# Feed-forward weights asked for during the gather of experts' rows, or behind its last row

## The chip, the core and the metric

One core of a Trainium2 chip runs the whole program in one launch. The metric is the device time in microseconds (us), the median of several executions. Engines: PE is TensorE's matmul, PEld its weight load, DVE is VectorE, ACT is ScalarE, POOL is GpSimd, SP is SyncE. SP's and POOL's queues issue DMA transfers; all of them run on the same 16 DMA engines.

## What is computed

A two-layer transformer block is followed by another two-layer block, on 256 tokens of width 1024, in float32. The part that matters here is the expert layer at the end of the first block and the feed-forward layer at the start of the second:

```python
def peer_ffn(h, w_q, sub_keys, down, up):          # per block of tokens
    q = (xb @ w_q).reshape(n, PEER_HEADS, 2, PEER_DHALF)
    ...                                            # top 16 of 128*128 experts, for each of 8 heads
    u = jnp.take(down, idx, axis=0)
    act = jax.nn.gelu(jnp.einsum('thkd,td->thk', u, xb))
    v = jnp.take(up, idx, axis=0)
    return jnp.einsum('thk,thkd->td', (gate * act).astype(v.dtype), v)
...
    return rms_norm(x, final_g)                    # end of the first block
...
x = x + 0.5 * swiglu(rms_norm_2(x, ffn_norm[0, 0]), w_gate, w_up, w_down)   # start of the second
```

Every token needs 8 x 16 rows of `down` and of `up`, in each of the two layers.

## The kernel before, in words

**The experts (`experts`, lines 1129 to 2030).** The tables `down` and `up` lie side by side in DRAM as `peer_rows`, 2048 float32 for each expert. The work is a list of 515 slots. A slot is one head, one of the two tiles of 128 tokens and one of the 16 picks: POOL issues one indirect DMA (L1337) that gathers 128 rows of 8 KB, 1 MB, into one of eight places of the ring `rows` (`ROW_SLOTS`). DVE takes the dot product of the `down` half with the normed tokens (L1894), ACT makes gelu, times the gate, times the identity (L1642, L1646, L1651), and PE multiplies the resulting diagonal with the `up` half into PSUM (L1484). When PE has done so, POOL may fetch the next row into that place. Layer 0's slots come first, then layer 1's (from `NEXT`); the last 32 slots of each head carry, in between, the query products, key scores and top-16 search (`route`) of the next head. `finish` (L1838, L1840) adds the sums of a tile to `x`.

**The weight ring (`Weights`, lines 190 to 219).** All large weights pass through a ring of six blocks of 1 MB (`SLOTS`). `W.issue(sp, n)` lets SP issue the blocks up to number n - 1, in order; before block b it waits until PE has counted block b - 5 as multiplied. Layer 1's eight query blocks (`b1` to `b1 + 7`) go through the ring, and behind them the feed-forward blocks: `b_next` = `b1 + 8` is the first gate block g0, then u0, g1, u1, d0, g2, u2, d1 and so on (gate, up, down). `W.issue(sp, b1 + PH + SLOTS)` (L1306) asks for six of them, g0 to g2, each when PE is done with one more query block.

**Splitting.** A float32 block is used as a high half (`fp32r`, copied by ACT, 1.9 us) and a low half (block minus high, by DVE, 2.3 us). Those of g0 and u0 are made within the loop over the slots: high at slots `total - 17` and `total - 9` (L1755), low at `total - 15` and `total - 7` (L2020), into the buffers `halves_a` and `halves_b`, which are free when all queries are done.

**The seam.** `experts` ends its own `nc.Block()`, and all engines meet there before `second_block_start` begins the next one. In it SP first loads the row `final_g`, the head gains and the position bias (1.5 MB) and then goes on with the ring (`layers[0].issue`). PE transposes x and starts on g0. ACT writes the high half of the transposed x (L2111), DVE the low one (L2117); then ACT and DVE take the final norm of x (L2965, behind a wait for all three loads), split g1 (L2168, L2173), and DVE makes the factor that PE spreads over the partitions behind u0 (L2321, L2266). A block of PE's work there takes some 5.6 us, and PE is busy without a break until the next seam.

Of the kernel before, what the change touches and what calls it, by code (L numbers as in the profile page):

```python
# [16 lines left out]
F32 = mybir.dt.float32  # L17
U32 = mybir.dt.uint32
F32R = mybir.dt.float32r
ALU = mybir.AluOpType  # L20
# [7 lines left out]
KD = D // P  # L28
# [12 lines left out]
PH = 8  # L41
# [19 lines left out]
SLOTS = 6  # L61
SPLIT_SLOTS = 3
ROW_SLOTS = 8
# [1065 lines left out]
def experts(kit, dram, rows, vec, late_bias, shared, first_root):  # L1129
# [16 lines left out]
    nc, W = kit.nc, kit.weights  # L1146
# [12 lines left out]
    total, per_head = len(slots), NT * TOPK  # L1159
    OTHER, PAST = NEXT + EARLY * TOPK, PH + EARLY  # L1160
    turns = [(0, hh, BOTH) for hh in range(PH)] + [(1, hh, (T,)) for hh, T in singles]
# [12 lines left out]
    split_block = list(range(PH)) + [PH + 4, PH + 5, PH + 6, PH + 5, PH + 4] + [PH + 4 + hh for hh in range(EARLY, PH)]  # L1174
# [5 lines left out]
    b0 = W.used  # L1180
    b_edge, b_bands, b_pool, b_late, b1 = (b0 + PH + i for i in range(5))
    b_next = b1 + PH
    NEXT_HIGH_AT, NEXT_LOW_AT = (total - 17, total - 9), (total - 15, total - 7)
    row_landed = [kit.count(f"row_landed{i}") for i in range(ROW_SLOTS)]
    (loaded, squares, normed, turned, high, low, high_made, split, queried, emptied, scored, copied, topped, shifted, exped,
     chosen, gated, dotted, gelued, scaled, weighed, summed) = (kit.count(n) for n in (
# [25 lines left out]
    with kit.sb("rows", [P, ROW_SLOTS, 2 * D]) as ring, kit.sb("keysT", [P, 2, P]) as keysT, \  # L1212
# [52 lines left out]
        @block.sync  # L1265
        def _(sp):
            keys_in.up(sp.dma_start(keysT[:], dram["peer_keysT"][0]), 16)
            W.issue(sp, b0 + SLOTS)
            for n in range(late):
                if n == ROW_SLOTS - 1:  # L1270
                    sp.wait_ge(rows.stored.sem, 16 * len(rows.LINES))
                rows.load_late(sp, n, ring)
            sp.wait_ge(cleared.sem, 3)
            rows.biased.up(sp.dma_start(late_line[0:P:32], late_bias), 16)
            for v in range(len(rows.LATE)):
                rows.store_late(sp, v, late_line[:, v])
            sp.wait_ge(normed.sem, n0 + NT)
            sp.wait_ge(rows.stored.sem, 16 * (len(rows.LINES) + len(rows.LATE)))
            sp.wait_ge(cleared.sem, 5)
            late_in.up(sp.dma_start(factors[0:64:32], row_of(1)), 16)  # L1280
            late_in.up(sp.dma_start(factors[64:P:32], row_of(4)), 16)
            late_in.up(sp.dma_start(plain[0:64:32], dram["pool_rows"]), 16)
            late_in.up(sp.dma_start(plain[64:P:32], row_of(0)), 16)
            late_in.up(sp.dma_start(row_stage[0:64:32], row_of(2)), 16)
            late_in.up(sp.dma_start(row_stage[64:P:32], row_of(3)), 16)
            edge_moved.up(sp.dma_start(dram["edge_h"], h[SHORT:P, 0]), 16)
            W.issue(sp, b_edge + 1)
            sp.wait_ge(edge_moved.sem, 16)
            edge_moved.up(sp.dma_start(edge_h, dram["edge_h"].rearrange("t (o n) -> t o n", o=1).to_broadcast([HALO, TOPK, D])), 16)
            W.issue(sp, b_late + 1)  # L1290
            sp.wait_ge(consumed.sem, 1)
            late_in.up(sp.dma_start(row_stage[0:64:32], row_of(5)), 16)
            sp.wait_ge(scored.sem, sc0 + PH)
            keys_in.up(sp.dma_start(keysT[:], dram["peer_keysT"][1]), 16)
            W.issue(sp, b1 + EARLY - 1)
            g = group_of[0, PH - 1, 0]
            sp.wait_ge(chosen.sem, ch0 + g + 1)
            sp.wait_ge(gated.sem, ga0 + g + 1)
            for name, a in (("edge_idx", idx), ("edge_gate", gate)):
                edge_moved.up(sp.dma_start(dram[name].rearrange("h t k -> t h k"),  # L1300
                                           a[SHORT:P, 0, edge_picks].rearrange("p (h k) -> p h k", h=EARLY)), 16)
            sp.wait_ge(edge_moved.sem, 64)
            for name, a in (("edge_idx", edge_idx.bitcast(U32)), ("edge_gate", edge_gate)):
                edge_moved.up(sp.dma_start(a, dram[name].rearrange("h t k -> (t k) h"), allow_slow_non_contiguous=True), 16)
            W.issue(sp, b1 + EARLY)
            W.issue(sp, b1 + PH + SLOTS)  # L1306
            sp.wait_ge(scored.sem, sc0 + len(turns))
            tables_in.up(sp.dma_start(onehot, dram["onehot"]), 16)
            tables_in.up(sp.dma_start(table[0:N_BUCKETS, :], dram["rel_bias_2"]), 16)
            sp.wait_ge(row_copied.sem, 2 * len(SPREAD) + DIL_GROUPS)  # L1310
            kit.load(sp, dram["bias_scratch"].rearrange("(g j) n -> j g n", g=DIL_GROUPS), bias_rows)
            sp.wait_ge(loaded.sem, loaded.n)

        @block.gpsimd
        def _(pool):
# [239 lines left out]
        def _(act):  # L1555
# [46 lines left out]
            def square(T, behind):  # L1602
                act.wait_ge(updated.sem, behind)
                kit.act(nc.scalar.activation(out, x[:, T], ACT.Square, accum_out=ss[:, 0, T:T + 1]))

            def root(a, b):
                squares.up(nc.scalar.activation(ss[:, 1, a:b], ss[:, 0, a:b], ACT.Sqrt, scale=1.0 / D, bias=kit.eps))

# [23 lines left out]
            for j, (L, hh, T, k, kind) in enumerate(slots):  # L1632
# [109 lines left out]
                for ahead, i in heads_at(c, EARLY + 1):  # L1742
# [5 lines left out]
                        take_scores(PAST + ahead)  # L1748
                    if i == AT["exp"] + per_head:
                        exp(PAST + 1 + ahead)  # L1750
                if j in NEXT_HIGH_AT:
                    i = NEXT_HIGH_AT.index(j)
                    W.wait(act, b_next + i)
                    act.wait_ge(W.multiplied, b_next)
                    nc.scalar.copy((w_high, x_high)[i], W.ring[:, (b_next + i) % SLOTS, :]).then_inc(high_made.sem, 1)  # L1755
                if c == 6 * per_head + 12:
                    for g, bank in enumerate((0, 1, 3)):
                        act.wait_ge(rowed.sem, 2 * len(SPREAD) + g + 1)
                        row_copied.up(nc.scalar.copy(bias_rows[:, g, :], kit.bank[bank][0:J, :]))

        @block.vector
        def _(dve):
# [83 lines left out]
            def modulate(dst, T, factor, offset):  # L1846
                kit.dve(nc.vector.scalar_tensor_tensor(out=dst, in0=x[:, T], scalar=ss[:, 2, T:T + 1],
                                                       in1=factor, op0=ALU.mult, op1=ALU.mult))
                return nc.vector.tensor_tensor(dst, dst, offset, ALU.add)

            def mix(T):

# [32 lines left out]
            for j, (L, hh, T, k, kind) in enumerate(slots):  # L1885
# [126 lines left out]
                if c == 6 * per_head + 4:  # L2012

                    dve.wait_ge(scored.sem, sc0 + len(turns))
                    consumed.up(nc.vector.memset(table[N_BUCKETS:N_BUCKETS + 1, :], NEG))
                if j in NEXT_LOW_AT:
                    i = NEXT_LOW_AT.index(j)
                    dve.wait_ge(high_made.sem, hm0 + len(split_block) + i + 1)
                    dve.wait_ge(W.multiplied, b_next)
                    nc.vector.tensor_tensor((w_low, x_low)[i], W.ring[:, (b_next + i) % SLOTS, :], (w_high, x_high)[i].bitcast(F32),  # L2020
                                            ALU.subtract).then_inc(split.sem, 1)
                if j == total - TOPK + 5:
                    dve.wait_ge(row_copied.sem, 12)
                    finish(0, total - TOPK - 1, gain1)
# [739 lines left out]
def second_block_start(kit, dram, shared, block):  # L2764
# [11 lines left out]
    with contextlib.ExitStack() as stack:  # L2776
# [162 lines left out]
        def _(dve):  # L2939
# [17 lines left out]
            dve.wait_ge(kit.count("gains_landed").sem, 16)  # L2957
            nc.vector.tensor_tensor(gain[:], kit.gains[:, 0], kit.gains[:, 6], ALU.mult).then_inc(made.sem, 1)
            dve.wait_ge(made.sem, m0 + 1)
            turns[0].make_low(dve, range(KD))  # L2960
            dve.wait_ge(rooted.sem, r0 + 1)
            kit.dve(nc.vector.reciprocal(ss[:, 2], ss[:, 1]))
            dve.wait_ge(loaded.sem, l0 + 48)
# [1172 lines left out]
```

## Time and profile before

| what | us |
|---|---|
| median of 3 runs | 2682.25 (2679.51 to 2684.45) |
| the profiled execution: its own time | 2681.42 |
| its span in the profile | 2679.5 |
| PE / DVE / ACT / POOL busy in the span | 2372.6 / 1851.5 / 1219.6 / 646.5 |

The span is measured from the first to the last recorded instruction; 1.9 us of the execution's own time lie outside it. The page cuts the span into 40 slices of 67 us and gives for each the busy share of every engine, the clock that TensorE was granted, and the busy share and rate of the DMA engines. The rows of experts fill slices 4 to 23, the second block the rest. PE's 89% is an average over stages with different limits, so the stage is read by itself.

### The profile page before, as it was taken

Reading aid. Unit: us, or ns where it says so; the run is one execution under the profiler, and the core shown is the slowest. Engines: PE = TensorE matmul, PEld = TensorE weight load, DVE = VectorE, ACT = ScalarE, POOL = GpSimd, SP = SyncE. Lnnn points to the kernel's source line nnn. Section 1 sums busy time; section 2 is a strip of 40 time slices with the busy share of each in tenths; the row PEclk is TensorE's granted clock in tenths of the full one; section 3 lists DMA queues with packets and bytes.
Section 4 is the critical chain, followed back from the end, with each engine's and each line's share of the span. In section 5 each row is a group of like instructions: output and inputs, shape, how many; then the busy total and the mean of one; then the engine's idle time right before and its main releaser. Section 6 shows DMA issues by size and latency. Waiting matters only on the chain. (4 is left out here: it accounts for less than half of the span.)

```text
span 2679.5 us, 35243 instructions
## 1 busy us (share of the span) xinstructions
PE 2372.6 (89%) x12936; PEld 1579.1 (59%) x12936; DVE 1851.5 (69%) x3447; ACT 1219.6 (46%) x2595; POOL 646.5 (24%) x547
## 2 busy tenths in 40 slices
PE   6988788888888988888778799999999998978999
PEld 4774333433334444333333268898888887856887
DVE  4777776678667776867764666676666666797665
ACT  3443434444445544444434454456445444445543
POOL 0004444454444434455444400000000000003000
PEclk8998999999999999999999999999999998988999
DMA  9799999999999999999999945542555554313553
GB/s 390 282 387 421 403 426 427 426 427 422 425 407 415 384 421 419 426 427 427 427 424 427 427 169 187 183 160 98 173 188 178 186 187 169 117 47 117 187 185 113
DMA packets 121705, 811.26 MB, mean 303 GB/s; under 512 B 15713, under 2 KB 18825, under 8 KB 26584
## 3 DMA queue, kind: packets, MB, share of 16 engines
q0 software_dynamic: 74160, 540.05, 48.2%
q1 hardware_dynamic: 47400, 269.32, 28.0%
q8 instruction: 85, 1.39, 0.2%
q14 instruction: 60, 0.49, 0.1%
HBM read 807.12 MB, written 1.15 MB: 302 GB/s over the span
## 5 line engine op out<-in xcount | busy, mean ns | idle before, releaser
L1484 PE MATMUL bank<-rows,diag 128*128 128x512 f32 (+1 forms) x2060 | 994.7, 620 | 210.0 <-ACT diag L1651 209.4
L1894 DVE CUSTOM_DVE_ANT_0 rows<-rows,h 128x1024 f32<-128x1024 f32 (+1 forms) x512 | 620.3, 1225 | 362.5 <-DMA rows<-in_peer_rows,idx 359.5
L1484 PEld LDWEIGHTS bank<-rows,diag 128*128 128x128 f32 (+1 forms) x2060 | 372.3, 194 | 735.5 <-ACT diag L1651 414.4
L1337 POOL DMA_INDIRECT rows<-in_peer_rows,idx x512 | 611.0, 1193 | 737.8 <-PE bank L1484 680.1
L1642 ACT ACTIVATE picks<-picks 128x1 f32<-128x1 f32 (+1 forms) x512 | 103.3, 202 | 634.5 <-DVE picks L1894 627.0
L2239 PE MATMUL bank<-hT_pair,halves 128*128 128x512 f32 x864 | 307.3, 399 | 0.4 <-DVE hT_pair L2117 0.4
L2240 PE MATMUL bank<-hT_pair,halves 128*128 128x256 f32 x864 | 242.3, 280 | 0.0
L1651 ACT ACTIVATE diag<-const_table,picks 128x128 f32<-128x128 f32 (+1 forms) x512 | 205.5, 401 | 48.0 <-ACT picks L1646 0.7
L2173 DVE TENSOR_TENSOR halves<-weight_ring,halves 128x2048 fp32r<-128x2048 f32 x73 | 167.0, 2289 | 72.0 <-ACT halves L2168 71.8
L2239 PEld LDWEIGHTS bank<-hT_pair,halves 128*128 128x128 f32 x864 | 162.3, 188 | 40.9 <-DVE hT_pair L2117 1.0
L1369 PE MATMUL bank<-halves_b,halves_a 128*128 128x256 f32 x864 | 165.9, 334 | 0.0
L2240 PEld LDWEIGHTS bank<-hT_pair,halves 128*128 128x128 f32 x864 | 163.1, 189 | 0.8
L1646 ACT ACTIVATE picks<-picks 128x1 f32<-128x1 f32 (+1 forms) x512 | 150.8, 295 | 18.5
L2168 ACT CAST halves<-weight_ring 128x2048 fp32r<-128x2048 f32 x73 | 139.4, 1911 | 42.2 <-PE bank L2248 27.0
L1369 PEld LDWEIGHTS bank<-halves_b,halves_a 128*128 128x128 f32 x864 | 119.1, 190 | 55.3 <-issue 55.3
L2173 DVE TENSOR_TENSOR halves_b<-weight_ring,halves_b 128x2048 fp32r<-128x2048 f32 x36 | 82.5, 2292 | 63.9 <-ACT halves_b L2168 63.9
L2239 PE MATMUL bank<-hT_pair,halves_b 128*128 128x512 f32 x336 | 119.6, 399 | 1.5 <-DVE work L2349 1.5
L3850 POOL MEMSET weight_ring<- 128x1024 f32 x1 | 1.0, 952 | 497.3 <-PE bank L3122 497.3
L2248 PE MATMUL bank<-halves_a,hidden 128*128 128x512 f32 x320 | 103.7, 395 | 0.0
L2173 DVE TENSOR_TENSOR halves_a<-weight_ring,halves_a 128x2048 fp32r<-128x2048 f32 x36 | 82.4, 2289 | 25.1 <-ACT halves_a L2168 25.1
L2168 ACT CAST halves_a<-weight_ring 128x2048 fp32r<-128x2048 f32 x36 | 68.9, 1915 | 59.7 <-PE bank L2248 57.8
L2240 PE MATMUL bank<-hT_pair,halves_b 128*128 128x256 f32 x336 | 94.2, 281 | 0.0
(601 smaller groups left out, 3784.8 us busy)
## 6 DMA issues: line engine op xcount, KB each, us to landing
weight_ring<-in_ffn_w_gate SPq DMA_DIRECT2D x44, 1024.0 KB, 4.8
weight_ring<-in_ffn_w_up SPq DMA_DIRECT2D x44, 1024.0 KB, 4.8
weight_ring<-in_ffn_w_down SPq DMA_DIRECT2D x44, 1024.0 KB, 4.8
mod_ring<-in_mod_w SPq DMA_DIRECT2D x16, 1024.0 KB, 8.7
weight_ring<-in_peer_w_q SPq DMA_DIRECT2D x16, 1024.0 KB, 11.4
half_ring<-in_mod_w SPq DMA_DIRECT2D x24, 512.0 KB, 6.8
rows<-in_mod_w SPq DMA_DIRECT2D x12, 1024.0 KB, 11.4
weight_ring<-in_attn_w_in SPq DMA_DIRECT2D x12, 1024.0 KB, 4.8
```

Source lines behind the costliest of these rows:

```text
L1337: nc.gpsimd.indirect_dma_start(ring[:, s], None, dram["peer_rows"], bass.IndirectOffsetOnAxis(ap=idx[:, T, n:n + 1], axis=0)).then_inc(row ...
L1369: mm = nc.tensor.matmul(kit.bank[hh % 2][:, half * SEQ:(half + 1) * SEQ], w[:, k, half * P:(half + 1) * P], t[:, :, k, :], start=(k == 0 a ...
L1484: mm = nc.tensor.matmul(bank[:, :], diag[0:n, j % DIAG_SLOTS], ring[0:n, j % ROW_SLOTS, D + half * 512:D + (half + 1) * 512], start=(j in ...
L1642: gelued.up(nc.scalar.activation(its_dot, its_dot, ACT.Gelu_apprx_tanh))
L1646: scaled.up(nc.scalar.activation(its_weight, its_dot, ACT.Copy, scale=its_gate))
L1651: weighed.up(nc.scalar.activation(diag[r, j % DIAG_SLOTS], eye[r], ACT.Copy, scale=its_weight))
L1894: dotted.up(nc.vector.tensor_tensor_reduce(out=ring[r, s, 0:D], in0=ring[r, s, 0:D], in1=its_h, scale=1.0, scalar=0.0, op0=ALU.mult, op1=A ...
L2168: self.kit.nc.scalar.copy(hi, w).then_inc(self.high_made.sem, 1)
L2173: self.kit.nc.vector.tensor_tensor(lo, w, hi.bitcast(F32), ALU.subtract).then_inc(self.split.sem, 1)
L2239: nc.tensor.matmul(bank[:, :], w_hi[:, k, cols], halves.pair[:, k, :], start=(k == 0), stop=False, skip_group_check=True)
L2240: mm = nc.tensor.matmul(bank[:, SEQ:2 * SEQ], w_lo[:, k, cols], halves.hi[:, k, :], start=False, stop=(k == KD - 1), skip_group_check=True)
L2248: mm = self.kit.nc.tensor.matmul(self.kit.bank[4 + 2 * T + half][:, :], hidden[:, f % 2, s, T * P:(T + 1) * P], w[:, s, half * 512:(half + ...
```

## The change

Only g0 is still fetched during the rows. SP then waits until the last row has landed and issues u0, g1, u1 and d0; g2 follows behind the three loads of the next Block. The high half of u0 is made by ACT after its last slot (`next_high(1)`), its low half by DVE in the next Block, between the first four and the last four columns of the transposed x. The diff, cut to what does something:

```diff
-    NEXT_HIGH_AT, NEXT_LOW_AT = (total - 17, total - 9), (total - 15, total - 7)
+    NEXT_HIGH_AT, NEXT_LOW_AT = total - 17, total - 15
...
             W.issue(sp, b1 + EARLY)
-            W.issue(sp, b1 + PH + SLOTS)
+            W.issue(sp, b1 + PH + 1)
             sp.wait_ge(scored.sem, sc0 + len(turns))
...
             sp.wait_ge(loaded.sem, loaded.n)
+            last = (total - 1) % ROW_SLOTS
+            sp.wait_ge(row_landed[last].sem, L0[last] + 16 * ((total - 1) // ROW_SLOTS + 1))
+            W.issue(sp, b_next + 5)
...
+            def next_high(i):
+                W.wait(act, b_next + i)
+                act.wait_ge(W.multiplied, b_next)
+                nc.scalar.copy((w_high, x_high)[i], W.ring[:, (b_next + i) % SLOTS, :]).then_inc(high_made.sem, 1)
...
-                if j in NEXT_HIGH_AT:
-                    i = NEXT_HIGH_AT.index(j)
-                    W.wait(act, b_next + i)
-                    act.wait_ge(W.multiplied, b_next)
-                    nc.scalar.copy((w_high, x_high)[i], W.ring[:, (b_next + i) % SLOTS, :]).then_inc(high_made.sem, 1)
+                if j == NEXT_HIGH_AT:
+                    next_high(0)
...
+            next_high(1)
...
+            def next_low():
+                dve.wait_ge(high_made.sem, hm0 + len(split_block) + 1)
+                dve.wait_ge(W.multiplied, b_next)
+                nc.vector.tensor_tensor(w_low, W.ring[:, b_next % SLOTS, :], w_high.bitcast(F32), ALU.subtract).then_inc(split.sem, 1)
...
-                if j in NEXT_LOW_AT:
...
+                if j == NEXT_LOW_AT:
+                    next_low()
...
-            turns[0].make_low(dve, range(KD))
+            turns[0].make_low(dve, range(4))
+            layers[0].make_low(dve, 1)
+            turns[0].make_low(dve, range(4, KD))
```

## Rows read from the trace of the kernel before

**Rows 1.** The page, 40 slices of 67 us: DMA busy tenths, then GB/s.

```profile
DMA  9799999999999999999999945542555554313553
GB/s 390 282 387 421 403 426 427 426 427 422 425 407 415 384 421 419 426 427 427 427 424 427 427 169 187 183 160 98 173 188 178 186 187 169 117 47 117 187 185 113
```

**Rows 2.** Windows of layer 1's rows: us, busy us, PEclk, DMA share, GB/s.

```profile
1075.00:1100.00 25.00, 17.70 (x49) 7.62 (x48) 24.38 (x78) 8.57 (x28) 10.71 (x8) 1.00 1.01 426
1112.88:1192.92 80.04, 66.72 (x189) 30.46 (x188) 57.50 (x137) 35.52 (x107) 39.49 (x33) 1.00 1.01 427
...
1425.00:1450.00 25.00, 21.13 (x46) 8.05 (x46) 11.94 (x19) 10.20 (x32) 13.07 (x12) 1.00 1.01 426
```

**Rows 3.** Timeline of SyncE's queue: start us, us, what it issued.

```profile
1024.23 0.43 SPq L214 DMA_DIRECT2D weight_ring<-in_ffn_w_gate  x1
1058.32 0.33 SPq L214 DMA_DIRECT2D weight_ring<-in_ffn_w_up  x1
...
1353.52 0.33 SPq L214 DMA_DIRECT2D weight_ring<-in_ffn_w_gate  x1
```

**Rows 4.** Row gathers (L1337) issued in 1100:1150 us, then in 1450:1550.

```profile
DMA to landing us min/median/max: 10.6/13.5/15.8
...
DMA to landing us min/median/max: 13.7/15.0/15.0
```

**Rows 5.** Timeline of the last rows and the seam.

```profile
1532.28 1.88 ACT L1755 CAST halves_b<-weight_ring 128x2048 fp32r<-128x2048 f32 x1
...
1536.13 2.29 DVE L2020 TENSOR_TENSOR halves_b<-weight_ring,halves_b 128x2048 fp32r<-128x2048 f32 x1
...
1547.26 1.23 DVE L1894 CUSTOM_DVE_ANT_0 rows<-rows,h 128x1024 f32<-128x1024 f32 x1 [1.25 <-DMA rows<-in_peer_rows,idx]
...
1549.70 1.23 DVE L1894 CUSTOM_DVE_ANT_0 rows<-rows,h 128x1024 f32<-128x1024 f32 x1 [1.21 <-DMA rows<-in_peer_rows,idx]
...
1552.05 1.98 PE L1484 MATMUL bank<-rows,diag 128*128 128x512 f32 x4 [0.46 <-ACT diag L1651]
...
1554.07 1.29 DVE L1838 TENSOR_TENSOR hT<-bank,vectors 128x512 f32<-128x512 f32 x2 [3.13 <-PE bank L1484]
1555.39 1.23 DVE L1840 TENSOR_TENSOR x_res<-x_res,hT 128x1024 f32<-128x1024 f32 x1
1557.13 0.36 SPq L187 DMA_DIRECT2D work<-in_final_g  x1
...
1557.17 1.06 PE L2104 MATMUL bank<-const_table,x_res 128*128 128x128 f32 x8 [3.14 <-PEq L1216]
```

**Rows 6.** Blocks issued back to back near 2446 us: first, fourth.

```profile
L214 SPq DMA_DIRECT2D weight_ring<-in_rw_wo x1: 350/350/350, 2446.3 to 2446.3; - x1
...
DMA to landing us min/median/max: 4.9/4.9/4.9
...
L214 SPq DMA_DIRECT2D weight_ring<-in_rw_wo x1: 752/752/752, 2447.6 to 2447.6; - x1
...
DMA to landing us min/median/max: 10.9/10.9/10.9
```

**Rows 7.** Windows of the next Block's start, columns as before.

```profile
1562.00:1564.00 2.00, 2.00 (x9) 1.81 (x8) 0.56 (x2) 1.43 (x4) 0.00 (x0) 0.50 1.08 382
...
1566.00:1568.00 2.00, 2.00 (x13) 1.73 (x12) 0.01 (x1) 1.97 (x5) 0.00 (x0) 1.00 0.00 1
```

**Rows 8.** Timeline of VectorE, and one row of TensorE, at the next Block.

```profile
1563.44 1.66 DVE L2117 SCALAR_TENSOR_TENSOR hT_pair<-bank,joined_gain,hT_pair 128x256 fp32r<-128x256 f32 x4 [2.72 <-ACT hT_pair L2111]
...
1568.20 2.48 DVE L2965 SCALAR_TENSOR_TENSOR x_res<-x_res,ss,work 128x1024 f32<-128x1024 f32 x2
1570.60 2.29 DVE L2173 TENSOR_TENSOR halves<-weight_ring,halves 128x2048 fp32r<-128x2048 f32 x1
...
1573.26 0.49 DVE L2321 TENSOR_SCALAR spread_factor<-const_table,factors 128x128 f32<-128x128 f32 x2
...
1574.62 0.60 PE L2266 MATMUL bank<-spread_factor,ones 128*128 128x128 f32 x4
```

More of the change, by code:

```diff
@@ L2015, in _ @@
                     consumed.up(nc.vector.memset(table[N_BUCKETS:N_BUCKETS + 1, :], NEG))
-                if j in NEXT_LOW_AT:
[L2017 to L2021, printed above, removed]
+                if j == NEXT_LOW_AT:
+                    next_low()
                 if j == total - TOPK + 5:
```

## The prediction

> **What bounds the kernel now.** I read the page's slices first: where the rows are gathered, the DMA engines are busy throughout at 422 to 427 GB/s, in the slices on either side of the last one before the seam as in the others, and the rate falls below 190 when the second block starts [rows 1]. The windows of layer 1's rows say the same at a finer grain: DMA share 1.01 and 426 or 427 GB/s, whether DVE is nearly full (24.38 of 25 us), PE works on queries, or no weight block is under way (1425 to 1450). Over one whole head, 80.0 us, PE is busy 66.7 us and DVE 57.5 [rows 2]. The gather is so paced by bytes moved. A block or a row of 1,048,576 bytes costs 1.0486 MB / 427 GB/s = 2.46 us of that pace, and the last rows are indeed taken up 1547.26, 1549.70: 2.44 us apart, each time after a wait for DMA [rows 5].
>
> SP's queue shows where the feed-forward blocks fall: g0 at 1024.23, u0 at 1058.32, then g1, u1, d0, and g2 last at 1353.52 [rows 3]. All five that move are issued inside the stretch in which the DMA engines never pause.
>
> At the seam the order of things is: last row taken up by DVE at 1549.70, its last matmuls 1552.05 to 1554.03, `finish` on DVE to 1556.62, all engines meet, first transposes 1557.17 [rows 5]. From there PE is the bound for the rest of the kernel.
>
> **Removed from the gather: five fetches.** 5 x 2.46 = 12.3 us, if the time that they leave is filled with rows. It is, if the queue of rows is never empty. The ring holds eight rows; a gather issued in the last stretch lands after 13.7 to 15.0 us, and where route and queries hold the ring back, after 10.6 at the least [rows 4]. Alone a 1 MB block lands in 4.9 us [rows 6]. So even there 10.6 - 4.9 = 5.7 us of other work stood ahead of the row, and one block less takes away 2.46 of it: 3.2 remain. PE and DVE could go as fast: a head without a weight block is 32 rows, 32 x 2.46 = 78.6 us, against 66.7 us of PE and 57.5 of DVE [rows 2]. The bounds are 0 (nothing refilled) and 12.3; nearest is the whole, since no row shows a pause. I take 12.3.
>
> Here a rule can be weighed. The Trainium skill (DMA: Bandwidth & Descriptors, Rules for kernel authors) says to issue a DMA early, compute, and wait late, so that its fixed cost is covered; this change does the reverse. What the rule would make of it is the third rival below. The same page of the skill (Specifications) puts HBM's share for one core at about 358 GB/s; the windows show 427 sustained, and by 358 five blocks would be 14.6 us instead of 12.3. The measurement decides.
>
> **Removed from the slots: one split.** ACT's cast at 1532.28 (1.88 us) and DVE's subtraction at 1536.13 (2.29 us) no longer stand between slots [rows 5]. Rows 1547.26 and 1549.70 still waited for DMA, so this cover is complete: 0. Without that cover it would be worth up to 2.3.
>
> **Added: SP's wait for the last row, four issues behind it.** Behind the wait on SP stands nothing but these and the end of the Block; SP's earlier loads of this Block are done. Times here are in the clock of the trace before; all of it shifts with the rows. SP wakes with DVE, at about 1549.7, and issues u0 at about 1549.8. The trace has four blocks issued back to back on a quiet queue: the first lands after 4.9 us, the fourth, issued 1.4 us later, after 10.9, so 12.3 after the first issue [rows 6], that is in order and 2.46 apart. u0 then lands at 1554.7, g1 at 1557.2, u1 at 1559.6, d0 at 1562.1. The four issues take about 2 us, over long before the engines meet.
>
> **Moved: u0's high half to the end of ACT's part.** It starts when u0 has landed: 1554.7 + 1.9 = 1556.6, and DVE's `finish` ends at 1556.62 [rows 5]. The meeting moves by 0.0; the bounds are 0 and 1 us (landing later than those 4.9).
>
> **Moved: u0's low half into the next Block.** 2.29 us on DVE, between L2117's two groups. DVE stood idle 2.72 us there, from 1560.72 to 1563.44, waiting for ACT [rows 8]. It fits with 0.4 to spare: 0. If it did not fit it would hold back the last four columns, and PE with them, by up to 2.3. The half itself is ready at 1563.0; PE wants it when g0's products end, about 5.6 us before the spread at 1574.62, so at 1569.
>
> **What is late next: the loads of the next Block.** SP issues `final_g` at 1557.13 and the gains and bias right behind [rows 5]. Their data was over by 1566, when the window shows 1 GB/s [rows 7]. Now it stands behind u1 and d0 in the same queue: d0's data ends about 1 us before it lands, at 1561, where before the loads could start at 1558. That is 3 us later (bounds 2 and 5): landed at 1569 to 1571 where DVE wanted all three at 1568.20 for L2965 [rows 8]. So DVE is held d = 0.5 to 2.9 us, I take 1.5. Behind it on DVE stand g1's low half and the factor, ready at 1573.75; PE's spread takes the factor up at 1574.62 [rows 8]. So 0.9 is cover and the stall on PE is d - 0.9: 0 to 2.0, value 0.6. g1's low half (end 1572.89 + d) is wanted only behind the spread, u1, d0 and g2 are wanted over 5 us later each; d0 and g2 have landed by then. 0 for these.
>
> **The clock.** PE stands for 3.14 us at the seam, and its granted clock is 0.50 (1.2 GHz) at 1562 to 1564, back at 1.00 (2.4 GHz) from 1566 [rows 5, 7]. The idle stretch ahead stays as long as it was, so I take the same course: 0. It can go otherwise: some 6 us at half clock are 3 us of work, given back if it doesn't fall.
>
> **Sum.** -12.3 (five fetches) + 0 (splits) + 0 (meeting) + 0.6 (loads of the next Block) = -11.7. The profiled span goes from 2679.5 to 2667.8 and its own time from 2681.42 to 2669.7. The median of the runs is 0.8 above the profiled execution: 2682.25 - 11.7 = 2670.5.
>
> **Rivals.**
> First, a gather that pauses. Where queries and route delay the ring, the DMA engines run dry once 2.46 us of weights are gone, and half of the gain is lost: -12.3 + 6.2 + 0.6 = -5.5, 2676.7. For it: DVE at 24.38 of 25 us in one window. Against: the 3.2 us still queued, and the stretch from 1425 on, without blocks, at full rate. 10%.
>
> Second, the four fetches share the engines instead of going in order, and u0 lands with d0, at 12.3 after the issue: 1562.1, cast to 1564.0, the meeting 7.4 us late, net -4.9: 2677.3. Against it: blocks of one queue landed 4.9 and 12.3 after the first issue. 8%.
>
> Third, the change does not do what it says, because the fetches cost the rows nothing and are only uncovered now: 0 + 0.6, 2682.9, no difference. This is what the rule of the skill quoted above amounts to. Against: a full DMA share in all windows of the gather. 5%.
>
> Fourth, the clock does not fall at the seam: 3 us more, -14.7, 2667.5. 6%.
>
> Fifth, on the other side: the loads behind the blocks. The position bias goes in runs of 1 KB, 1536 of them. If each took a turn as long as an 8 KB run of a block (8192 B x 16 / 427 GB/s = 0.31 us, 96 on each engine, 29 us), it would land at about 1591 and DVE would be held 22.8 us: -12.3 + 22.8 - 0.9 = +9.6, 2691.9. It decides from a delay of 12.3 + 5.4 + 0.9 = 18.6 us on. Against: alone they were through in 8 us, and in one queue they come after the blocks, not among them. 2%.
>
> **How the numbers follow.** The forecast has the remaining 69%, with a range of its own from 2670 (no stall) to 2673 (stall 2.0 and meeting 1 late). The whole range runs from the fourth rival to just past the first, 2666.5 to 2677: 85% of the chances lie in it, without the second, third and fifth. A measurement of this kernel tells a change from none at 0.2%, 5.4 us: faster 0.93 (forecast, first, second, fourth), same 0.05, slower 0.02.
>
> **What would show it.** Layer 1's windows stay at 426 or 427 GB/s, and the last row is taken up at 1549.7 - 12.3 = 1537.4. SP issues four blocks at 1537.5 to 1539.5, the first lands after 4.9 us. Transposes begin 12.3 us earlier, at 1544.9, and each us less is a us that the gather paused or the meeting waited. L2965 begins 0.5 to 2.9 us later against them than before, behind a wait for DMA, and PE's L2266 starts 12.3 - 0.6 = 11.7 earlier, at 1562.9. The prediction is wrong if a window of the gather shows less than 420 GB/s, if u0's cast ends over 1 us behind `finish`, or if L2965 waits for DMA by more than 3 us.

## The result, and the profile after

The changed kernel takes 2669.30 us in the median of 7 runs (2667.27 to 2674.21), against 2682.97 us (2679.51 to 2685.88) of the kernel before on the same chip, 7 runs: 13.7 us less. The ratio is 0.9950, 95% interval 0.9940 to 0.9959, or 11.0 to 16.1 us. The prediction was 11.7 us less, 2670.5, with a range from 2666.5 to 2677. Its profiled execution takes 2669.8 us, with a span of 2667.9 where 2667.8 was forecast.

The page of the changed kernel, its slices of the span, DMA busy tenths and GB/s (answers to [rows 1]):

```profile
DMA  9799999999999999999999965542555554213553
GB/s 383 283 386 415 403 427 427 426 427 422 425 412 420 374 426 406 426 427 427 427 423 427 427 232 188 188 158 95 183 183 186 185 184 177 105 50 118 185 187 112
```

The gather looks as it did; slice 24, with 232 GB/s where 169 stood, now holds the blocks that moved behind the last row. Windows of layer 1's rows, columns as in [rows 2]:

```profile
1075.00:1100.00 25.00, 17.71 (x48) 7.59 (x47) 24.38 (x78) 8.80 (x28) 10.69 (x8) 1.00 1.01 427
...
1125.00:1150.00 25.00, 17.54 (x40) 6.69 (x38) 24.33 (x77) 8.52 (x30) 11.32 (x11) 1.00 1.01 426
1425.00:1450.00 25.00, 19.22 (x40) 6.77 (x40) 12.22 (x19) 8.79 (x30) 9.32 (x10) 1.00 1.01 427
```

Still 426 or 427 GB/s, though g1, asked for at 1112.88 before, is no longer fetched there; the DMA engines found rows to fetch instead. Over the whole way from g0's issue to the last row both kernels have a mean of 422 GB/s. Even where DVE was busy 24.38 of 25 us the rate did not fall. So the gather ends when its bytes are through, and there are fewer of them.

The last rows and the seam in the changed kernel's timeline (answers to [rows 5]; L1905 is the dot product, L1487 the row's matmul, L1612 the cast of u0, L2111 the transposes):

```profile
1537.19 1.23 DVE L1905 CUSTOM_DVE_ANT_0 rows<-rows,h 128x1024 f32<-128x1024 f32 x1 [1.22 <-DMA rows<-in_peer_rows,idx]
...
1539.63 1.23 DVE L1905 CUSTOM_DVE_ANT_0 rows<-rows,h 128x1024 f32<-128x1024 f32 x1 [1.21 <-DMA rows<-in_peer_rows,idx]
1539.66 0.35 SPq L214 DMA_DIRECT2D weight_ring<-in_ffn_w_up  x1
...
1541.00 0.62 SPq L214 DMA_DIRECT2D weight_ring<-in_ffn_w_down  x1
...
1541.98 1.98 PE L1487 MATMUL bank<-rows,diag 128*128 128x512 f32 x4 [0.46 <-ACT diag L1659]
...
1544.43 1.90 ACT L1612 CAST halves_b<-weight_ring 128x2048 fp32r<-128x2048 f32 x1 [2.51 <-DMA weight_ring<-in_ffn_w_up]
1545.32 1.23 DVE L1846 TENSOR_TENSOR x_res<-x_res,hT 128x1024 f32<-128x1024 f32 x1
1547.05 0.33 SPq L187 DMA_DIRECT2D work<-in_final_g  x1
...
1547.10 1.94 PE L2111 MATMUL bank<-const_table,x_res 128*128 128x128 f32 x8 [3.14 <-PEq L1216]
```

The last row is taken up at 1539.63, 10.07 us earlier than before [rows 5], and SP issues u0 in the same moment, 0.03 us later. ACT waited for u0 and began its cast 4.77 us behind the issue; the cast ends at 1546.33, `finish` at 1546.55, and the first transposes start at 1547.10. That is 7.47 us behind the last row, as in [rows 5].

VectorE's timeline behind the seam, and the two rows of TensorE at the factor spread (answers to [rows 8]; L2180 at 1551.23 is the low half of u0):

```profile
1551.23 2.28 DVE L2180 TENSOR_TENSOR halves_b<-weight_ring,halves_b 128x2048 fp32r<-128x2048 f32 x1
1554.04 1.66 DVE L2124 SCALAR_TENSOR_TENSOR hT_pair<-bank,joined_gain,hT_pair 128x256 fp32r<-128x256 f32 x4 [0.52 <-ACT hT_pair L2118]
1558.59 0.17 DVE L2971 RECIPROCAL ss<-ss 128x2 f32<-128x2 f32 x1 [2.89 <-ACT ss L2889]
1558.79 2.48 DVE L2974 SCALAR_TENSOR_TENSOR x_res<-x_res,ss,work 128x1024 f32<-128x1024 f32 x2
1561.19 2.29 DVE L2180 TENSOR_TENSOR halves<-weight_ring,halves 128x2048 fp32r<-128x2048 f32 x1
...
1563.85 0.48 DVE L2328 TENSOR_SCALAR spread_factor<-const_table,factors 128x128 f32<-128x128 f32 x2
```

```profile
1563.97 0.28 PE L2247 MATMUL bank<-hT_pair,halves_b 128*128 128x256 f32 x1
1564.38 0.71 PE L2273 MATMUL bank<-spread_factor,ones 128*128 128x128 f32 x4
```

u0's low half stands in the idle stretch between the two groups of L2124, and 0.52 us of idleness are left. The final norm (L2974) starts 0.03 us behind the reciprocal: no wait for DMA. The factor is ready at 1564.33, TensorE's last product of u0 has ended at 1564.25, and the spread starts at 1564.38. Before, the spread began 0.12 us after the start of the product ahead of it (1574.50, 1574.62), now 0.41: TensorE waited some 0.3 us for the factor.

The kernel's other parts vary from one execution to the next, the stretches that the change leaves alone too: in this pair the rows ran 1.4 us late already at 1025, and the second half of the kernel made up 1.4 us. Over all the kernels below, the way from the factor spread to the end takes 1101.4 to 1111.5 us, with the same instructions in it. For a finer measure than the whole time I take, from the one profiled execution of each kernel, the way from a mark in the gather that all kernels share, the first of the last six query blocks issued by SP, to the last row's dot product. The mark in the timeline of the kernel before, and in that of the changed one:

```profile
762.16 180.23 SPq L214 DMA_DIRECT2D weight_ring<-in_peer_w_q  x4
```

```profile
763.65 181.39 SPq L214 DMA_DIRECT2D weight_ring<-in_peer_w_q  x4
```

Before: 1549.70 - 762.16 = 787.54 us. Changed: 1539.63 - 763.65 = 775.98, so 11.56 less. The second measure is the seam, from the last row's dot product to the factor spread: 1574.62 - 1549.70 = 24.92 before [rows 5, 8], 1564.38 - 1539.63 = 24.75 now.

### The profile page after: what moved, and what is told of

It reads as the page before. It is cut to its first block and busy times, and to the rows that moved or that the text cites. A ratio compares the mean times of both kernels' runs of the same rounds, so it can differ in the third digit from the quotient of the medians.

```text
span 2667.9 us, 35241 instructions
## 1 busy us (share of the span) xinstructions
PE 2367.8 (89%) x12935; PEld 1577.4 (59%) x12936; DVE 1850.8 (69%) x3447; ACT 1219.5 (46%) x2595; POOL 645.7 (24%) x547
## 5 line engine op out<-in xcount | busy, mean ns | idle before, releaser
L1487 PE MATMUL bank<-rows,diag 128*128 128x512 f32 (+1 forms) x2060 | 990.9, 618 | 201.9 <-ACT diag L1659 201.0
L1905 DVE CUSTOM_DVE_ANT_0 rows<-rows,h 128x1024 f32<-128x1024 f32 (+1 forms) x512 | 620.0, 1224 | 354.2 <-DMA rows<-in_peer_rows,idx 348.2
L1487 PEld LDWEIGHTS bank<-rows,diag 128*128 128x128 f32 (+1 forms) x2060 | 371.4, 194 | 724.5 <-ACT diag L1659 404.0
L2180 DVE TENSOR_TENSOR halves<-weight_ring,halves 128x2048 fp32r<-128x2048 f32 x73 | 166.9, 2288 | 72.2 <-ACT halves L2175 72.1
L2180 DVE TENSOR_TENSOR halves_b<-weight_ring,halves_b 128x2048 fp32r<-128x2048 f32 x37 | 84.8, 2291 | 63.8 <-ACT halves_b L2175 63.8
L2180 DVE TENSOR_TENSOR halves_a<-weight_ring,halves_a 128x2048 fp32r<-128x2048 f32 x36 | 82.4, 2289 | 25.0 <-ACT halves_a L2175 25.0
## 6 DMA issues: line engine op xcount, KB each, us to landing
weight_ring<-in_peer_w_q SPq DMA_DIRECT2D x16, 1024.0 KB, 10.7
```

Source lines behind the costliest of these rows:

```text
L1487: mm = nc.tensor.matmul(bank[:, :], diag[0:n, j % DIAG_SLOTS], ring[0:n, j % ROW_SLOTS, D + half * 512:D + (half + 1) * 512], start=(j in ...
L1905: dotted.up(nc.vector.tensor_tensor_reduce(out=ring[r, s, 0:D], in0=ring[r, s, 0:D], in1=its_h, scale=1.0, scalar=0.0, op0=ALU.mult, op1=A ...
L2180: self.kit.nc.vector.tensor_tensor(lo, w, hi.bitcast(F32), ALU.subtract).then_inc(self.split.sem, 1)
```

## The experiments

Each was timed beside the kernel before on the same chip, in three sets on three chips: the first has small_in_rows, extra_in_rows, small_at_seam and three_moved, the third changed_again, loads_between and six_between_again, the second the others; the changed kernel's own comparison stands above. Ratios of different sets are compared through the kernel before. The table has the megabytes of feed-forward weights that are fetched between the mark and the last row, the two measures from each kernel's one profiled execution, and the ratio from the timed runs with its 95% interval.

| kernel | MB in the gather | mark to last row, us | seam, us | ratio |
|---|---|---|---|---|
| before | 6 | 787.54 | 24.92 | 1 |
| split_only | 6 | 788.80 | 24.37 | 0.9995 (0.9985 to 1.0005) |
| extra_in_rows | 11 | 799.41 | 24.68 | 1.0046 (1.0033 to 1.0058) |
| asked_early | 5 | 784.18 | 24.47 | 0.9993 (0.9983 to 1.0003) |
| three_moved | 3 | 781.58 | 24.43 | 0.9967 (0.9954 to 0.9980) |
| small_in_rows | 1.3 | 774.33 | 24.75 | 0.9967 (0.9955 to 0.9979) |
| changed | 1 | 775.98 | 24.75 | 0.9950 (0.9940 to 0.9959) |
| changed_again | 1 | 776.30 | 24.75 | 0.9962 (0.9949 to 0.9975) |
| loads_between | 1 | 776.55 | 24.77 | 0.9957 (0.9942 to 0.9972) |
| small_at_seam | 1 | 774.80 | 24.76 | 0.9949 (0.9936 to 0.9961) |
| six_moved | 0 | 773.58 | 28.02 | 0.9954 (0.9941 to 0.9967) |
| six_between | 0 | 773.69 | 25.50 | 0.9950 (0.9937 to 0.9963) |
| six_between_again | 0 | 773.78 | 25.52 | 0.9952 (0.9939 to 0.9965) |

**1. The five fetches cut small, in the rows (small_in_rows).**

```diff
+            if b in self.small:
+                dst, src = dst[:, 0:1, 0:128], src[:, 0:1, 0:128]
             sp.dma_start(dst, src).then_inc(self.landed[b % SLOTS], 16)
...
+    W.small = range(b_next + 1, b_next + 6)
```

> The kernel before, with its five fetches u0, g1, u1, d0, g2 still asked for during the rows and split where they were, but each cut to 64 KB (128 columns of 512 bytes); the rest of each block is left out of the computation. Theory A (the gather pays for bytes, 2.46 us for each MB): 5 x 2.46 x 15/16 = 11.5 us faster than before, ratio 0.9957, rows at 427 GB/s to the end. Rival B (the gather pauses where queries and route hold the ring back, so half is lost): some 6 us faster, 0.998, and windows under 420 GB/s. Rival C (the fetches were hidden): no difference.

Measured: 0.9967, which is 8.9 us less (5.6 to 12.1), and the last row 13.2 us nearer to the mark. The 11.5 us of theory A lie in the interval, no difference (C) does not. By the ratio alone the 6 us of B could not be told from A; the windows of its gather, 425 or 426 GB/s from 1100 to 1500 us, speak against it, and so does the first measure. The two measures differ: the last row gained 13.2 us and the seam took 24.75, but the way from the spread to the end took 1111.5 us in this profiled execution, 6.6 more than before. The runs don't show why.

**2. The five fetches doubled (extra_in_rows).**

```diff
+            if b in self.twice:
+                self.first.up(sp.dma_start(dst, src), 16)
+                sp.wait_ge(self.first.sem, self.first.n)
             sp.dma_start(dst, src).then_inc(self.landed[b % SLOTS], 16)
...
+            W.twice, W.first = range(b_next + 1, b_next + 6), edge_moved
```

> The kernel before with the five fetches doubled: each of u0, g1, u1, d0, g2 is fetched once, SP waits until it has landed, and is fetched again into the same place. 5 MB more during the rows, nothing else changed. Theory A: 12.3 us slower, ratio 1.0046. Rival B: also 12.3 slower, since more bytes leave no pause. Rival C: no difference.

Measured: 1.0046, 12.3 us more (8.9 to 15.6), as worked out; the first measure has 11.9 more. The windows of its gather, columns as in [rows 2]:

```profile
1100.00:1200.00 100.00, 85.59 (x254) 40.64 (x253) 70.59 (x163) 44.96 (x131) 48.84 (x40) 0.98 1.01 427
1200.00:1300.00 100.00, 80.00 (x216) 35.72 (x214) 63.38 (x148) 38.45 (x117) 49.78 (x39) 0.97 1.01 427
1300.00:1400.00 100.00, 79.23 (x204) 34.87 (x204) 69.51 (x182) 38.02 (x116) 47.84 (x37) 0.95 1.01 424
```

They stand at the same 424 to 427 GB/s as before. A fetch during the rows had to be paid for, though no engine waited for it. This ends rival C.

**3. The five fetches cut small, at the seam (small_at_seam).** The edit of experiment 1 in the changed kernel.

> The changed kernel with u0, g1, u1, d0, g2 cut to 64 KB each where they are asked for now, behind the last row; the rest of each block is left out of the computation. It shows what the fetches cost at the seam. Theory A with nothing exposed there: as the changed kernel, 13 us faster than before in this comparison (0.995), within 1 us of it, and the way from the last row to TensorE's factor spread 24.5 us in place of the changed kernel's 24.75. Rival D (the fetches at the seam cost 1 to 3 us by holding back the meeting and the loads of the next Block): that much faster than the changed kernel, 0.9945 or less.

Measured: 0.9949, against 0.9950, and a seam of 24.76 us against 24.75. The ratio alone would leave room for rival D: its interval, 0.9936 to 0.9961, holds 0.9945. The seam does not: with four whole blocks behind the last row and g2 behind the loads it takes 24.75 us, with 64 KB of each 24.76. So rival D falls by the seam of the profiled executions. The 24.5 us that were expected did not come either; the 0.3 us of waiting for the factor are there without the blocks too, and belong to the clock (see below).

**4. Three blocks moved and not five (three_moved).**

```diff
-            W.issue(sp, b1 + PH + 1)
+            W.issue(sp, b1 + PH + 3)
```

> The changed kernel, but u0 and g1 are asked for during the rows again, so that three blocks move and not five; u0 is still split at the seam. Theory A: 3 x 2.46 = 7.4 us faster than before, ratio 0.9972, last row 7.4 earlier. Rival E (the gain comes from the split of u0 that no longer stands between the slots, or from the clock at the seam, and not from the bytes): the whole 12 to 13 us stay, 0.995.

Measured: 0.9967, 8.9 us less (5.4 to 12.3), expected 7.4. The last row is 6.0 us nearer to the mark than before, where 7.4 were expected. The interval overlaps that of the full change, so the ratio alone doesn't settle E; the first measure, 5.6 us short of the changed kernel's, does in part, and the next experiment does it directly.

**5. Only the split moved (split_only).**

```diff
-            W.issue(sp, b1 + PH + 1)
+            W.issue(sp, b1 + PH + SLOTS)
...
-            last = (total - 1) % ROW_SLOTS
-            sp.wait_ge(row_landed[last].sem, L0[last] + 16 * ((total - 1) // ROW_SLOTS + 1))
-            W.issue(sp, b_next + 5)
```

> The fetches as in the kernel before, all six during the rows and no wait of SP for the last row; only the split of u0 is at the seam, as in the changed kernel. Theory A (the gather pays for bytes): no difference to before, 1.000, last row where it was; DVE's 2.3 us fit into its idle stretch at the seam. Rival E (the split between the slots was what cost): several us of the gain are here already, 0.998 or less.

Measured: 0.9995 (0.9985 to 1.0005) in 12 runs: no difference that is clear of noise, at most 4.0 us of gain, and the last row is no nearer to the mark (788.80 against 787.54). Rival E wanted 0.998 or less and falls: neither between the slots nor at the seam did the split of u0 cost anything that these runs show.

**6. The blocks asked for six rows early (asked_early).**

```diff
-            last = (total - 1) % ROW_SLOTS
-            sp.wait_ge(row_landed[last].sem, L0[last] + 16 * ((total - 1) // ROW_SLOTS + 1))
+            last = (total - 7) % ROW_SLOTS
+            sp.wait_ge(row_landed[last].sem, L0[last] + 16 * ((total - 7) // ROW_SLOTS + 1))
```

> The changed kernel, but SP waits only for the seventh slot from the end, so u0, g1, u1 and d0 are asked for with six rows still queued. Theory A: these 4 MB go before the last row's end again, the last row lands some 9.8 us later than in the changed kernel, only g2 is still saved: 2.5 us faster than before, 0.999. Rival F (the DMA engines have spare time at the end of the gather, since their busy share falls over the last 5 us, and take the blocks in that time): most of the gain stays, 0.996.

Measured: 0.9993, 1.9 us less (-0.8 to 4.6), where theory A has 2.5 and F 10.7. SP's first and fourth issue in its timeline, and the dot products of some of the last rows:

```profile
1523.22 0.35 SPq L214 DMA_DIRECT2D weight_ring<-in_ffn_w_up  x1
...
1524.56 0.43 SPq L214 DMA_DIRECT2D weight_ring<-in_ffn_w_down  x1
```

```profile
1523.19 1.23 DVE L1905 CUSTOM_DVE_ANT_0 rows<-rows,h 128x1024 f32<-128x1024 f32 x1 [1.21 <-DMA rows<-in_peer_rows,idx]
...
1525.63 1.23 DVE L1905 CUSTOM_DVE_ANT_0 rows<-rows,h 128x1024 f32<-128x1024 f32 x1 [1.21 <-DMA rows<-in_peer_rows,idx]
...
1529.33 1.23 DVE L1905 CUSTOM_DVE_ANT_0 rows<-rows,h 128x1024 f32<-128x1024 f32 x1 [2.46 <-DMA rows<-in_peer_rows,idx]
...
1534.22 1.22 DVE L1905 CUSTOM_DVE_ANT_0 rows<-rows,h 128x1024 f32<-128x1024 f32 x1 [3.65 <-DMA rows<-in_peer_rows,idx]
...
1539.14 1.23 DVE L1905 CUSTOM_DVE_ANT_0 rows<-rows,h 128x1024 f32<-128x1024 f32 x1 [3.69 <-DMA rows<-in_peer_rows,idx]
...
1544.03 1.22 DVE L1905 CUSTOM_DVE_ANT_0 rows<-rows,h 128x1024 f32<-128x1024 f32 x1 [3.65 <-DMA rows<-in_peer_rows,idx]
...
1547.70 1.22 DVE L1905 CUSTOM_DVE_ANT_0 rows<-rows,h 128x1024 f32<-128x1024 f32 x1 [2.44 <-DMA rows<-in_peer_rows,idx]
```

Before the issue the rows came 2.44 us apart. With the blocks under way they are taken up at 1529.33, 1534.22, 1539.14 and 1544.03, 4.9 us apart: SP's queue and POOL's share the engines half and half. The steps from 1525.63 to the last row are 3.70, 4.89, 4.92, 4.89 and 3.67; less 2.44 each, that is 9.87 us of delay within one trace, for four blocks of 2.46 (9.84). This version is the changed kernel but for the moment at which it asks, and its last row is 8.2 us later by the first measure, which spans 780 us and scatters more.

This refutes F for six rows. Its premise holds, though: in the changed kernel the DMA engines are nearly idle over the last 4 us before the last row is taken up at 1539.63, columns as in [rows 2]:

```profile
1534.00:1536.00 2.00, 1.54 (x4) 0.68 (x4) 1.23 (x2) 0.49 (x2) 0.00 (x0) 1.00 0.57 242
1536.00:1538.00 2.00, 1.54 (x4) 0.49 (x3) 0.81 (x1) 0.90 (x3) 0.00 (x0) 1.00 0.15 61
1538.00:1540.00 2.00, 1.53 (x4) 0.49 (x3) 0.79 (x3) 0.90 (x3) 0.00 (x0) 1.00 0.06 25
```

What it would give to ask one or two rows early, into that time, no run shows.

**7. The sixth block too (six_moved).** g0 is also asked for behind the last row. The edit is cut to its main lines; left out is that PE's first transposes no longer stand behind the wait for g0's split:

```diff
-            W.issue(sp, b1 + PH + 1)
+            W.issue(sp, b1 + PH)
...
-            next_high(1)
+            next_high(0)
...
-            turns[0].make_high(act, range(KD))
+            turns[0].make_high(act, range(4))
+            layers[0].make_high(act, 1)
+            turns[0].make_high(act, range(4, KD))
...
-            turns[0].make_low(dve, range(4))
+            layers[0].make_low(dve, 0)
+            turns[0].make_low(dve, range(KD))
             layers[0].make_low(dve, 1)
-            turns[0].make_low(dve, range(4, KD))
```

> The changed kernel with g0 moved too: all six blocks behind the last row, g0's high half by ACT at the end of the experts, its low half first on DVE in the next Block, u0's high between the two groups of transposed columns, u0's low behind them; PE's first transposes no longer wait for g0's split. Theory A: last row another 2.46 us earlier, the seam longer by 0.6 (DVE's 2.3 us for g0's low half less the 1.7 it stood idle there) and up to 2 more where the next Block's loads now stand behind one block more: 12.6 to 14.2 faster than before, 0.9948 to 0.9953. Rival G (the first fetch is exposed in full at the seam): last row to factor spread longer by 3 us or more, no gain over the changed kernel or a loss.

Measured: 0.9954 (0.9941 to 0.9967), 12.3 us less, just short of the 12.6 to 14.2 expected. The last row came 2.3 us nearer to the mark (773.58, against 775.91 in the mean of the four kernels with 1 MB), but the seam grew by 3.3 us to 28.02. That is the size that rival G names; the timeline shows that it has another cause:

```profile
1542.71 1.94 PE L2106 MATMUL bank<-const_table,x_res 128*128 128x128 f32 x8 [3.14 <-PEq L1215]
1542.91 2.29 DVE L2175 TENSOR_TENSOR halves_a<-weight_ring,halves_a 128x2048 fp32r<-128x2048 f32 x1
1545.20 1.66 DVE L2119 SCALAR_TENSOR_TENSOR hT_pair<-bank,joined_gain,hT_pair 128x256 fp32r<-128x256 f32 x4
...
1554.19 0.17 DVE L2971 RECIPROCAL ss<-ss 128x2 f32<-128x2 f32 x1 [0.70 <-ACT ss L2889]
1557.66 2.48 DVE L2974 SCALAR_TENSOR_TENSOR x_res<-x_res,ss,work 128x1024 f32<-128x1024 f32 x2 [3.31 <-DMA bias<-bias_scratch]
```

The first fetch isn't exposed: the first transposes come 7.47 us behind the last row (1535.24), as in the changed kernel. Nor did g0's low half hold DVE up here: the reciprocal comes 11.48 us behind the transposes, in the changed kernel 11.49 (1547.10, 1558.59). All of the 3.3 us is the final norm, which started at 1557.66, behind a wait of 3.31 us for the position bias. One more block ahead of it in SP's queue makes the loads the last to arrive.

**8. u1, d0 and g2 behind the loads (six_between, and again; loads_between for the changed kernel).**

```diff
-            W.issue(sp, b_next + 5)
+            W.issue(sp, b_next + 3)
```

> As all six moved, but only g0, u0 and g1 are asked for ahead of the next Block's loads (final gain, head gains, position bias), and u1, d0, g2 behind them. If in the six-block version DVE waits for these loads, that wait is gone: 14.2 us faster than before, 0.9947. If it does not wait there, both are the same.

The same place in the six-block version with this edit, and then in the changed kernel with it:

```profile
1556.29 0.17 DVE L2971 RECIPROCAL ss<-ss 128x2 f32<-128x2 f32 x1 [0.70 <-ACT ss L2889]
1556.49 2.48 DVE L2974 SCALAR_TENSOR_TENSOR x_res<-x_res,ss,work 128x1024 f32<-128x1024 f32 x2
```

```profile
1558.07 0.17 DVE L2971 RECIPROCAL ss<-ss 128x2 f32<-128x2 f32 x1 [2.90 <-ACT ss L2889]
1558.27 2.48 DVE L2974 SCALAR_TENSOR_TENSOR x_res<-x_res,ss,work 128x1024 f32<-128x1024 f32 x2
```

The wait is gone, and the six-block seam is 25.50 us, 0.75 over the changed kernel's. Here the transposes take 1.06 us, and g0's low half does hold the first L2119 up: it starts at 1547.30, 2.41 us behind them, where L2117 started 1.89 behind [rows 5] before (1559.06). The ratio is 0.9950 (0.9937 to 0.9963), 13.4 us less where 14.2 were worked out, and 0.9952 when run again.

> The changed kernel once more, beside the two below. 12 to 13 us faster than before, 0.9950 to 0.9955; from the last row to TensorE's factor spread some 24.6 us.

> The changed kernel, but u1 and d0 are asked for behind the next Block's loads and only u0 and g1 ahead of them. The loads now land some 5 us earlier. In the changed kernel DVE started on the final norm without waiting for them, so this should change nothing: same time as the changed kernel. If the loads do hold DVE up in most executions, as the prediction took it (0.6 us of stall), it is up to 1 us faster.

> All six blocks moved, u1, d0 and g2 behind the next Block's loads, once more. By the bytes 2.46 us less in the gather than the changed kernel and by the first run 0.75 us more at the seam: 1.7 us faster than the changed kernel beside it, 0.9944 against 0.9950.

In the changed kernel the edit alone changes nothing: L2974 follows the reciprocal with it as without it, the seam is 24.77 against 24.75 us, and the ratio 0.9957 (0.9942 to 0.9972) against 0.9962 (0.9949 to 0.9975) of the changed kernel in the same set. That 0.9962, 10.2 us less, lies outside the 0.9950 to 0.9955 expected of it; its interval holds both. The six-block version, expected 1.7 us better (1.5 by the measures here: 2.23 in the gather less 0.75 at the seam), has a median of 2670.12 against 2671.67 beside it, and its interval, 0.9939 to 0.9965, overlaps that of the changed kernel. It can't be called faster. No version tried is shown to beat the changed kernel.

## Why the prediction was right, point by point

**The bound of the gather.** Right, though one reading was not: the DMA engines are not at 422 to 427 GB/s throughout. Seven of the twenty slices of the gather have less, down to 384 [rows 1]. They all end by 1072 us, and the first moved block was asked for at 1058; from there on the reading holds, and that is the part that the sum needs. Between 0 and 11 MB of weights the way from the mark to the last row grows from 773.7 to 799.4 us. From 6 to 1 MB it is 788.17 (mean of two kernels) less 775.91 (mean of four), 12.26 us, 2.45 a block, where the prediction had 2.46 and 12.3 in all. Other steps give less (11 to 6: 2.25 a block; 1 to 0: 2.23; asked early: 8.3 us for 4 blocks), and single kernels scatter by 1 to 2 us around a line; within one trace, asked_early has 2.47 a block.

**The queue of rows never empty.** Right where it mattered; 426 and 427 GB/s in the windows of layer 1, and the first rival's half gain did not come. The sign of being wrong, a window under 420 GB/s, was drawn too wide: the changed kernel has 405 from 1025 to 1050, where the kernel before has 421. But no moved block was fetched in that window before either, and split_only, with all six blocks in the rows, has 405 there too. From 1050 to 1530 the windows of 25 us of the changed kernel have 425 to 428 GB/s, except 417 from 1350 to 1375, where SP loads two small tables; the kernel before has 416 there.

**The splits, the meeting, u0's low half.** Each was put at 0 and came at 0 as far as the runs tell: split_only shows it for both splits together, the 7.47 us from the last row to the transposes for the meeting. The cast of u0 ended 0.22 us ahead of `finish`, where the prediction had them level, and of the 0.4 us to spare beside DVE's low half 0.52 were left.

**The loads of the next Block.** This term was mis-sized: 0.6 us of stall behind a delay of 1.5, and DVE did not wait for them at all. The step that failed is the time for the loads: I took their data to start 3 us later and to take as long as before. Windows of the kernel before and of the changed one, columns as in [rows 2]:

```profile
1556.00:1558.00 2.00, 0.83 (x8) 0.85 (x8) 0.79 (x2) 0.00 (x0) 0.00 (x0) 1.00 0.00 0
1558.00:1560.00 2.00, 0.63 (x4) 0.40 (x2) 0.94 (x3) 1.57 (x4) 0.00 (x0) 0.69 1.01 249
1560.00:1562.00 2.00, 2.00 (x9) 1.81 (x9) 0.72 (x2) 0.00 (x0) 0.00 (x0) 0.50 0.87 224
```

```profile
1546.00:1548.00 2.00, 0.90 (x5) 0.93 (x6) 0.71 (x2) 0.33 (x1) 0.00 (x0) 0.71 1.02 430
...
1552.00:1554.00 2.00, 2.00 (x11) 1.95 (x10) 1.52 (x1) 0.84 (x3) 0.00 (x0) 0.59 1.02 335
1554.00:1556.00 2.00, 2.00 (x14) 1.72 (x13) 1.66 (x4) 1.97 (x6) 0.00 (x0) 1.00 1.10 360
1556.00:1558.00 2.00, 2.00 (x14) 1.72 (x13) 0.00 (x0) 1.98 (x3) 0.00 (x0) 1.00 1.05 374
```

The windows don't tell transfers apart, but packet sizes do. `final_g` moves in 128 packets of 4 KB and the bias in 1536 of 1 KB; nothing else there has such packets. The DMA view of 1558.0 to 1566.1 of the kernel before, then of 1550.9 to 1557.7 of the changed one, has them all:

```profile
DMA packets 1841, 2.11 MB, mean 261 GB/s; under 512 B 176, under 2 KB 1712, under 8 KB 1840
```

```profile
DMA packets 1897, 2.43 MB, mean 358 GB/s; under 512 B 192, under 2 KB 1728, under 8 KB 1856
```

(1840 - 1712 = 128 and 1712 - 176 = 1536; 1856 - 1728 and 1728 - 192 give the same.) In steps of 0.2 us, the first 4 KB packet comes at 1558.1 before, 0.9 us behind the first transposes, and at 1550.9 now, 3.8 behind them: 2.9 later, as forecast. But the loads' data ran for 8.0 us before and for 6.8 now, so it ended only 1.7 us later against the transposes, outside the bounds of 2 and 5. (By its own lower bound the data would have been over at 1568, ahead of DVE's 1568.20, so a delay of 0 belonged into that range.) And DVE came to the final norm 11.69 us behind the transposes where it had been 11.03, 0.7 later, because of the clock. L2974 does start later by as much as the prediction's 0.5 to 2.9 allows, but not behind a wait for DMA: that match is luck.

It was close. In six_moved the wait ended 0.5 us behind the last of these packets; by that, the loads of the changed kernel landed at about 1558.2 (an estimate), 0.6 us ahead of L2974. With one more block the first 4 KB packet came 2.7 us later against the last row and the loads ran 8.0 us again, 1.2 longer: 2.7 + 1.2 - 0.6 = 3.3, the wait that was seen. So the place was right, and the 2 MB took less time than I gave them. Why, the runs don't show: over all kernels the loads take 6.6 (changed_again) to 9.2 us (asked_early).

**The clock.** I took its course to be the same. The windows show that it fell earlier: 0.71 on average at 1546 to 1548, where before it stood at 1.00 in the window of the first transposes; the eight transposes took 1.94 us in place of 1.06, and DVE's and ACT's chain began 0.67 us later. It was back at 1.00 (2.4 GHz) by 1554, 7 us behind the first transposes, where before it took 9 (1557.17 to 1566) [rows 5, 7]. The two nearly cancel: the factor spread comes 17.28 us behind the transposes, against 17.45. What is left of it is the 0.3 us for which TensorE waited for the factor. What moved the fall, the runs don't show; the moved blocks' traffic it is not, since small_at_seam, without it, has transposes of 1.94 us too. Between kernels the seam varies from 24.4 to 24.9 us with no order by what was fetched.

**The sum.** -11.7 was forecast. The profiled execution has -11.6, made of 1.37 us late by 1025 (before any moved block), -11.44 from there to the last row, -0.17 at the seam, and -1.4 in the rest, where nothing was changed. The medians say -13.7 and, of changed_again, -11.3 (the ratios 13.4 and 10.2). The difference between the two comparisons is as large as what the forecast was off.

That the profiled execution meets the forecast within 0.1 us is in part luck. The forecast had the last row at 1537.4, it came at 1539.63: 2.2 us late, 1.4 of it from ahead of the first moved block and 0.9 because the gather gained 11.44 and not 12.3. The stall of 0.6 did not come, and the rest of the kernel, where nothing was changed, happened to be 1.4 us shorter.

## What to carry to other kernels

Where a stage is paced by DMA bytes, a prefetch inside it isn't free, whatever idle engine seems to cover it: each block of 1 MB is paid at the stage's rate, here 2.46 us. Look for the point at which the stage's last transfer lands, count how long the engines still work on what has landed (here 7.5 us to the next Block and 11 more to TensorE's first use of u0), and ask there for the blocks that this time covers. A sixth block brought nothing more that the runs can tell: with it at the head of the queue the seam lost what the gather gained, and with the order changed it lost 0.75 of 2.23 us. When transfers go ahead of others in one queue, check what is queued behind: the loads of the next Block turned from never waited for to 3.3 us late with one block more.

## What the runs showed of the hardware

With both queues full, SP's and POOL's transfers alternated: the rows' interval went from 2.44 to 4.9 us while four blocks were under way. The Trainium skill (DMA: Bandwidth & Descriptors, Queues, rings and completion order) says that each DMA engine goes round the queues that have work for it, packet by packet; this trace agrees, with 4.9 us.

A block issued in a burst did not wait for those behind it: in the changed kernel u0 was there 4.8 us behind its issue at the latest (1539.66, 1544.43), with three others right behind it, and g1, issued at 1540.05, landed after 6.8 us, 2.4 behind u0.

The same three loads, 2 MB in small packets, took from 6.6 to 9.2 us from the first packet to the last. With whole blocks ahead of them in the queue they took 6.8 and 6.6 us in the two executions of the changed kernel, but 8.0 in six_moved; alone they took 8.0 in the kernel before.
